# Hybrid decoder layer: norm weights of the mixers moved into the merge's split of y, D times x on ScalarE, the transposes of B in another PSUM bank, the SSM means one level later

## The chip, the cores and the metric

The kernel runs on one core of one Trainium2 chip: TensorE (PE), VectorE (DVE), ScalarE (ACT), GpSimd (POOL), and DMA queues issued by SP, ACT and POOL. The metric is the device time of one execution in microseconds. Lower is better.

## The reference

One layer over 1024 tokens of width 1024, float32. What matters here is the token mixer: three branches on the projection of the normed input, whose results are merged by gates and projected.

```python
o = chunked_gated_linear_attention(q, k, v, log_a, GLA_CHUNK)      # GLA; HGRN2 is the same form
o = rms_norm(o, gla_norm_w.reshape(GLA_HEADS, GLA_DV)).reshape(bsz, t_len, GLA_VW)
y_gla = (o * jax.nn.silu(gr.astype(f32))).astype(dtype)
...
y = ssd_chunked_scan(xs, dt, a_neg, bm, cm, SSM_CHUNK)
y = y + ssm_d.astype(f32)[:, None] * xs
y = y.reshape(bsz, t_len, SSM_D_INNER) * jax.nn.silu(sz.astype(f32))
y = rms_norm(y.reshape(..., SSM_GROUPS, SSM_D_INNER // SSM_GROUPS), ssm_norm_w.reshape(...))
...
merged = g0 * (y_gla @ w_br_gla) + g1 * (y_hgrn @ w_br_hgrn) + g2 * (y_ssm @ w_br_ssm)
return merged @ w_out
```

`rms_norm(x, w)` is x times the inverse root of its mean square, times w. In `ssd_chunked_scan` each chunk of 128 tokens uses `w = decay * (C B^T) * dt` within the chunk, and a state that is scaled and gets `x B^T` added. After the mixer come a second norm, the router, 32 experts (top 2 of a group) and a last norm.

## The kernel before, in words

The program is a row of blocks: the first norm and decays, `project` (the input projection), `mixers`, `merge_and_route`, the experts, `finish`. Each block has one hand-written list of instructions for each engine, and semaphores between them; each engine works through its own list in order, so a wait holds up all that stands behind it.

**`mixers` (578 to 1086 us)** goes over 8 chunks of 128 tokens (`body(c)`). Channels lie on partitions. GLA and HGRN2 are computed by levels: for level 0 to 6 VectorE makes two factor tiles (`factors`, L1468 to L1470), TensorE multiplies them (`level`, L1627), VectorE copies the wanted part into `score` (`scores_in`, L1486). The SSM branch has B and C in `bc_in`, x in `x_in` (named `gate_raw_a` in the trace, as z is), the decay matrix `wmat` (named `dn_raw_a`). `wmat` is loaded by SP as a broadcast of the 16 heads' b to all partitions (`load_bb`, L1128, 1 MB), as soon as TensorE has used the old one; VectorE's L1517 is the first to read it.

Between these, TensorE's list has gate matmuls: `fill(8)` puts eight of the 128x512 matmuls (L1602) that project the merge's gates. Each 24 of them make a result of 512 columns ("head") in PSUM bank 7, which ScalarE evicts (`late`, L1258) and stores; ScalarE also rounds the next gate weights (`late_hi`, L1251) or issues their load (L1246), and VectorE makes their remainder (`late_lo`, L1375).

Work of chunk c that is finished during chunk c+1, in VectorE's order: the norm of o with the gate (L1439, L1443), the sum of the parts of y (L1400), D times x (L1405), the gate z (L1411); then ScalarE squares it (`ssm_squares`, L1283), TensorE averages the squares over the channels by a matmul with a constant matrix (`ssm_means`, L1657, in two parts), ScalarE turns the mean into the inverse root (`ssm_scale`, L1287 and L1289), and VectorE forms the result (`ssm_out`, L1454). The weights of both norms and D are columns, one number for each partition and each 128 channels, so L1443, L1405 and L1454 are eight instructions each.

TensorE's list around the place in question, in chunk c: level 3, `ssm_state(c-1)` (L1649, reads B transposed, `bT`), eight gate matmuls, `ssm_means(c-1)` (L1657, into bank 2), the four transposes of B (L1701, into bank 6), eight gate matmuls, level 4, eight gate matmuls, the eight transposes of x (L1710, into banks 2 and 3), level 5. Bank 6 holds C B^T before, which VectorE reads by L1523 (`cbm`), so L1701 waits for `cbm_ready`. ScalarE copies B transposed to SBUF by L1330, late in the chunk. L1710 waits for `ms2_read`: ScalarE must have read the means from bank 2.

**`merge_and_route`** starts behind a barrier. It loads y for half of the tokens in eight pieces of two 512-column groups. ScalarE rounds a piece to the upper part (`upper_y`, L2118), VectorE makes the remainder (`rest_y`, L2217), and TensorE multiplies both parts with the branches' weights (L2457), starting with piece 0. The second half's pieces are split during the output projection (L2478).

Of the kernel before, what the change touches and what calls it, by code (L numbers as in the profile page):

```python
# [17 lines left out]
P = 128  # L18
T = 1024
D = 1024  # L20
CH = 128
# [936 lines left out]
def mixers(nc, io, dr, h_hi, h_lo, l_raw, l_hi, l_lo, w_place, xz_place, stored, early):  # L958
# [10 lines left out]
    N_PAR = 5  # L969
# [4 lines left out]
    with ExitStack() as ctx:  # L974
# [35 lines left out]
        nw, nw_s, d_col = sb("nw", [P, NH]), sb("nw_s", [P, 8]), sb("d_col", [P, 8])  # L1010
# [69 lines left out]
        intra_used = sem("intra_used")  # L1080
        xd_ready = sem("xd_ready")
# [21 lines left out]
        def _(sp):  # L1103
# [61 lines left out]
            sp.dma_start(nw[:, 0:4], io["gla_norm_w"].rearrange("(k p) -> p k", p=P)).then_inc(par_in, 16)  # L1165
            sp.dma_start(nw[:, 4:8], io["hgrn_norm_w"].rearrange("(k p) -> p k", p=P)).then_inc(par_in, 16)
            sp.dma_start(nw_s[:], io["ssm_norm_w"].rearrange("(k p) -> p k", p=P)).then_inc(par_in, 16)
# [72 lines left out]
        def _(act):  # L1240
# [37 lines left out]

            def ssm_squares(c):
# [11 lines left out]
            def body(c):  # L1291
# [23 lines left out]
                late(h0 + 1)  # L1315
                if c:
                    ssm_scale(c - 1)
# [9 lines left out]
                act.wait_ge(bT_ps_ready, c + 1)  # L1327
                if c:
                    act.wait_ge(hupd_ready, c)
# [38 lines left out]
        def _(dve):  # L1368
# [68 lines left out]
            def gla_hgrn_out(c):  # L1437
# [132 lines left out]
            for c in range(NCH):  # L1570
                if c == 1:
# [1597 lines left out]
```

## Time and profile before

| | before |
|---|---|
| median of 3 runs | 2035.61 us |
| range of the runs | 2033.6 to 2041.8 us |
| span of the profiled execution | 2040.4 us |
| TensorE busy in the span | 1925.7 us, 94% |
| VectorE busy | 1472.5 us, 72% |
| ScalarE busy | 1048.0 us, 51% |
| mean granted TensorE clock | 0.975 |

The profiled execution is one of the kernel's; its span runs from its first to its last instruction, and the page gives no other time for it. Busy time of TensorE is modelled (matmuls overlap), so that 94% is not 94% of its peak. The granted clock is a share of 2.4 GHz; 0.5 is 1.2 GHz. From 1300 us on the DMA engines are nearly always busy (the experts' weights), before that TensorE is. A wait is put down to the event that came last. In rows of the order of time the first number is the start and the second the time until the last end; a name like `gate_raw_a` is that of the buffer, which x, z and y share.

### The profile page before, as it was taken

How to read it: one execution, taken by the hardware profiler on the slowest of the kernel's cores; microseconds unless marked ns; L12 is line 12 of the kernel's file. 1: busy time of each engine (PE TensorE's matmuls, PEld its weight loads, DVE VectorE, ACT ScalarE, POOL GpSimd, SP SyncE). 2: the span in 40 equal slices, each digit the busy share in tenths (PEclk: the TensorE clock that was granted, in tenths of full speed). 3: DMA queues.
4: the chain of work that ended last, by engine and by line, in shares of the span. 5: the costliest groups of instructions: out<-in, count | busy, mean ns of one | idle time of the engine just before them, and what ended most of it. 6: DMA issues, size and time to landing. Idle time of an engine off the chain costs nothing. (4 is left out here: it accounts for less than half of the span.)

```text
span 2040.4 us, 26797 instructions
## 1 busy us (share of the span) xinstructions
PE 1925.7 (94%) x10602; PEld 1576.7 (77%) x10603; DVE 1472.5 (72%) x1687; ACT 1048.0 (51%) x1234; POOL 218.3 (11%) x173
## 2 busy tenths in 40 slices
PE   6999999999999999999998999995999999999993
PEld 5789888888977777777776888874788888888881
DVE  5876467667227888788775656556889988999875
ACT  5234344444224545444444334223777887888763
POOL 3310000000030000000001000012122222222210
PEclk9999999999999999999998999997999999999996
DMA  5242332432355557656537654543999999999986
GB/s 168 86 145 73 114 104 97 131 104 93 107 145 158 151 160 168 167 127 152 160 115 282 206 204 182 229 178 138 349 376 384 389 386 385 389 386 387 387 331 259
DMA packets 212415, 436.11 MB, mean 214 GB/s; under 512 B 28018, under 2 KB 151042, under 8 KB 184770
## 3 DMA queue, kind: packets, MB, share of 16 engines
q1 hardware_dynamic: 179394, 355.68, 50.3%
q10 hardware_dynamic: 20864, 53.49, 7.5%
q0 software_dynamic: 12032, 25.22, 3.2%
q8 instruction: 85, 1.39, 0.3%
q14 instruction: 40, 0.33, 0.0%
HBM read 369.67 MB, written 81.43 MB: 221 GB/s over the span
## 5 line engine op out<-in xcount | busy, mean ns | idle before, releaser
L1602 PE MATMUL psum<-h_hi,l_hi 128*128 128x512 f32 x384 | 158.5, 413 | 4.9 <-PEq L58 3.3
L1602 PE MATMUL psum<-h_lo,l_hi 128*128 128x512 f32 x384 | 159.8, 416 | 0.0
L1602 PE MATMUL psum<-h_hi,l_lo 128*128 128x512 f32 x384 | 157.9, 411 | 0.0
L2741 DVE TENSOR_TENSOR gu_lo<-up_raw,gu_hi 128x2048 fp32r<-128x2048 f32 x64 | 146.3, 2288 | 13.2 <-ACT gu_hi L2684 13.2
L2684 ACT CAST gu_hi<-up_raw 128x2048 fp32r<-128x2048 f32 x64 | 122.1, 1909 | 35.0 <-PE u_ps L2813 35.0
L1258 ACT COPY l_out<-psum 128x512 f32<-128x512 f32 x48 | 28.1, 585 | 170.3 <-PE psum L1602 162.3
L2457 PE MATMUL mpsum<-y_hi,wb_hi 128*128 128x512 f32 x256 | 103.3, 403 | 10.1 <-DVE y_lo L2217 9.1
L2813 PE MATMUL g_ps<-gu_hi,xeT_hi 128*128 128x512 f32 x256 | 105.0, 410 | 5.8 <-DVE xeT_lo L2750 5.8
L806 DVE TENSOR_TENSOR w_lo<-w_raw,w_hi 128x512 fp32r<-128x512 f32 x90 | 61.9, 689 | 65.5 <-ACT w_hi L662 65.5
L662 ACT CAST w_hi<-w_raw 128x512 fp32r<-128x512 f32 x90 | 55.7, 622 | 91.9 <-PE ps L931 91.4
L2457 PE MATMUL mpsum<-y_lo,wb_hi 128*128 128x512 f32 x256 | 101.7, 397 | 0.0
L2457 PE MATMUL mpsum<-y_hi,wb_lo 128*128 128x512 f32 x256 | 101.6, 397 | 0.0
L2813 PE MATMUL g_ps<-gu_hi,xeT_lo 128*128 128x512 f32 x256 | 101.6, 397 | 0.0
L2813 PE MATMUL g_ps<-gu_lo,xeT_hi 128*128 128x512 f32 x256 | 101.4, 396 | 0.0
L2813 PE MATMUL u_ps<-gu_hi,xeT_lo 128*128 128x512 f32 x256 | 99.7, 389 | 0.0
L2813 PE MATMUL u_ps<-gu_hi,xeT_hi 128*128 128x512 f32 x256 | 99.6, 389 | 0.0
L2813 PE MATMUL u_ps<-gu_lo,xeT_hi 128*128 128x512 f32 x256 | 99.6, 389 | 0.0
L3123 POOL DMA_INDIRECT xe<-s_h,recs x32 | 88.6, 2770 | 32.4 <-PE xT_ps L2784 14.9
L1602 PEld LDWEIGHTS psum<-h_hi,l_hi 128*128 128x128 f32 x384 | 73.2, 191 | 21.9 <-issue 7.0
L2741 DVE TENSOR_TENSOR gu_lo<-gate_raw_a,gu_hi 128x2048 fp32r<-128x2048 f32 x32 | 73.4, 2293 | 22.2 <-ACT gu_hi L2684 22.2
L1602 PEld LDWEIGHTS psum<-h_hi,l_lo 128*128 128x128 f32 x384 | 73.5, 191 | 18.8 <-issue 3.3
L2662 POOL DMA_INDIRECT s_pairs<-ye,recs x32 | 41.4, 1293 | 431.3 <-ACT ye L2701 417.9
(465 smaller groups left out, 5419.0 us busy)
## 6 DMA issues: line engine op xcount, KB each, us to landing
up_raw<-moe SPq DMA_DIRECT2D x62, 1024.0 KB, 8.1
gate_raw_a<-moe SPq DMA_DIRECT2D x33, 1024.0 KB, 8.4
gate_raw<-moe SPq DMA_DIRECT2D x33, 1024.0 KB, 8.4
dn_raw_a<-moe SPq DMA_DIRECT2D x31, 1024.0 KB, 7.2
dn_raw<-moe SPq DMA_DIRECT2D x31, 1024.0 KB, 8.0
w_raw<-w_in SPq DMA_DIRECT2D x26, 1024.0 KB, 6.1
l_raw<-w_gates ACTq DMA_DIRECT2D x24, 512.0 KB, 5.4
s_gates<-l_out ACTq DMA_DIRECT2D x48, 256.0 KB, 4.0
```

The source lines that it names most:

```text
L662: nc.scalar.copy(slot_hi[g], source(n, g)).then_inc(hi_ready, 1)
L806: ins = tt(slot_lo[g], source(n, g), slot_hi[g].bitcast(F32), ALU.subtract).then_inc(split_ready, 1)
L1258: nc.scalar.copy(l_out[h % 2][:], psum[:, late_bank(h), :]).then_inc(l_evicted, 1)
L1602: ins = nc.tensor.matmul(psum[:, bank, :], w[t % 2][:, k, :], x[:, k, half * 512:half * 512 + 512], start=i == 0, stop=i == LATE_MM - 1, s ...
L2457: ins = nc.tensor.matmul(ps[:, br, :], w[:, k * P:(k + 1) * P], y[:, k, :], start=k == k0 and q == 0, stop=k == k1 - 1 and q == 2)
L2662: pool.indirect_dma_start(out=dr["pairs"], out_offset=bass.IndirectOffsetOnAxis(ap=recs[:, e, 1:2], axis=0), in_=ye[b][:], in_offset=None, ...
L2684: nc.scalar.copy(gu_hi[p][:], gu_raw[p][:]).then_inc(gu_hi_ready, 1)
L2741: nc.vector.tensor_tensor(gu_lo[p][:], gu_raw[p][:], gu_hi[p][:].bitcast(F32), ALU.subtract).then_inc(gu_ready, 1)
L2813: ins = nc.tensor.matmul(ps[:], x[:, (p - at) * GK + k, :], w[:, k, :], start=p == at and k == 0 and q == 0, stop=p == at + GU // 2 - 1 an ...
L3123: nc.gpsimd.indirect_dma_start(out=xe[e % 2][:], out_offset=None, in_=dr["h2"], in_offset=bass.IndirectOffsetOnAxis(ap=recs[:, e, 0:1], ax ...
```

## The change

- The weights of the GLA, HGRN2 and SSM norms leave the mixers. L1443 and L1454 become one multiplication of 1024 columns each. The weights are loaded into `y_weight`, a tile that lives on, and are applied where the merge splits y: the rounding on ScalarE takes them as its scale, the remainder on VectorE as its scalar. A piece is now two instructions of 512 columns on each of the two engines.
- D times x moves from VectorE (L1405) to ScalarE (`x_scaled`): eight activations in place in `x_in`, once x has been transposed. VectorE adds the product by one instruction.
- B is transposed into the second half of `mid_ps` (bank 3), not bank 6. L1701's wait for `cbm_ready` goes; a wait for `ms_read` comes. The copy of `bT` on ScalarE moves ahead of `ssm_scale`, and the wait for `bT_ready` on TensorE moves from `intra` to the transposes of x.
- `ssm_means` moves on TensorE from ahead of the transposes of B to behind level 4.

```diff
+            for (k0, k1), name in (((0, 4), "gla_norm_w"), ((4, 8), "hgrn_norm_w"), ((8, 16), "ssm_norm_w")):
+                sp.dma_start(y_weight[:, k0:k1], io[name].rearrange("(k p) -> p k", p=P)).then_inc(early["yw"], 16)
...
+            def x_scaled(c):
+                if c == 0:
+                    act.wait_ge(par_in, 16 * N_PAR)
+                act.wait_ge(xT_ready, c + 1)
+                for k in range(8):
+                    ins = nc.scalar.activation(x_in[:, k, :], x_in[:, k, :], ACT.Copy, scale=d_col[:, k:k + 1])
+                ins.then_inc(xs_ready, 1)
...
                 late(h0 + 1)
+                act.wait_ge(bT_ps_ready, c + 1)
+                if c:
+                    act.wait_ge(hupd_ready, c)
+                nc.scalar.copy(flat(bT[:]), mid_ps[:, 512:1024]).then_inc(bT_ready, 1)
                 if c:
                     ssm_scale(c - 1)
...
-                nc.scalar.copy(flat(bT[:]), ssm_ps).then_inc(bT_ready, 1)
...
                 late(h0 + 3)
+                x_scaled(c)
...
             def x_in_sum(c):
                 dve.wait_ge(intra_used, 2 * c + 2)
-                for k in range(8):
-                    ins = stt(yt[:, k, :], x_in[:, k, :], d_col[:, k:k + 1], yt[:, k, :], ALU.mult, ALU.add)
-                ins.then_inc(xd_ready, 1)
+                dve.wait_ge(xs_ready, c + 1)
+                tt(yt[:], x_in, yt[:], ALU.add).then_inc(xd_ready, 1)
...
-                for h in range(NH):
-                    ins = stt(ya[:, h, :], g_in[:, h, :], nw[:, h:h + 1], ya[:, h, :], ALU.mult, ALU.mult)
-                ins.then_inc(ya_ready, 1)
+                tt(ya, g_in[:], ya, ALU.mult).then_inc(ya_ready, 1)
...
-                for k in range(8):
-                    ins = stt(yb[:, k, :], yt[:, k, :], nw_s[:, k:k + 1], rs2[:, k // 2, :], ALU.mult, ALU.mult)
-                ins.then_inc(yb_ready, 1)
+                grouped = lambda x: x.rearrange("p (g a) t -> p g a t", a=2)
+                tt(grouped(yb), grouped(yt[:]), rs2[:].unsqueeze(2).to_broadcast([P, SSM_GROUPS, 2, CH]), ALU.mult).then_inc(yb_ready, 1)
...
                 fill(SLOT)
                 if c:
-                    ssm_means(c - 1)
-                pe.wait_ge(cbm_ready, c + 1)
+                    pe.wait_ge(ms_read, c)
                 for g in range(SSM_GROUPS):
-                    ins = nc.tensor.transpose(ssm_ps[:, g * P:(g + 1) * P], bc_in[:, g, :], ident[:])
+                    ins = nc.tensor.transpose(mid_ps[:, 512 + g * P:512 + (g + 1) * P], bc_in[:, g, :], ident[:])
                 ins.then_inc(bT_ps_ready, 1)
                 fill(SLOT)
                 level(c, 4)
+                if c:
+                    ssm_means(c - 1)
                 fill(SLOT)
                 pe.wait_ge(x_loaded, 16 * (c + 1))
+                pe.wait_ge(bT_ready, c + 1)
...
-                nc.scalar.copy(y_hi[:, q * PK:(q + 1) * PK, :], y_part(p)).then_inc(y_hi_ready, 1)
+                for a in range(PK):
+                    k = q * PK + a
+                    ins = nc.scalar.activation(y_hi[:, k, :], y_part(p)[:, a, :], ACT.Copy, scale=y_weight[:, k:k + 1])
+                ins.then_inc(y_hi_ready, 1)
...
-                tt(y_lo[:, ks, :], y_part(p), y_hi[:, ks, :].bitcast(F32), ALU.subtract).then_inc(y_ready, 1)
+                for a in range(PK):
+                    k = q * PK + a
+                    ins = stt(y_lo[:, k, :], y_part(p)[:, a, :], y_weight[:, k:k + 1], y_hi[:, k, :].bitcast(F32), ALU.mult, ALU.subtract)
+                ins.then_inc(y_ready, 1)
```

TensorE in the middle of a chunk, from level 3's last part to the transposes of x; the gate matmuls between are left out. Before:

```order
L1649 MATMUL psum<-xdt,bT 128x256 x3
...
L1657 MATMUL psum<-y_out,mean_b 128x512 [waits ms_read,sq2_ready]
L1657 MATMUL psum<-y_out,mean_b 128x512
L1701 MATMUL psum<-ident_m,bc_in 128x128 [waits cbm_ready]
L1701 MATMUL psum<-ident_m,bc_in 128x128 x3
...
L1627 MATMUL psum<-q_lv,k_lv 64x2x32 [waits score_ready,qk_ready]
...
L1710 MATMUL psum<-ident_m,gate_raw_a 128x128 [waits ms2_read,x_loaded]
```

And now:

```order
L1702 MATMUL psum<-ident_m,bc_in 128x128 [waits ms_read]
L1702 MATMUL psum<-ident_m,bc_in 128x128 x3
...
L1630 MATMUL psum<-q_lv,k_lv 64x2x32 [waits score_ready,qk_ready]
...
L1660 MATMUL psum<-y_out,mean_b 128x512 [waits ms_read,sq2_ready]
L1660 MATMUL psum<-y_out,mean_b 128x512
L1605 MATMUL psum<-h_hi,l_hi 128x512 [waits l_evicted,l_split]
...
L1714 MATMUL psum<-ident_m,gate_raw_a 128x128 [waits ms2_read,bT_ready,x_loaded]
```

The means stand behind level 4, right ahead of the gate matmuls that begin a new head, and L1714 has one wait more.

ScalarE in the same part of a chunk with an even number, from the differences (L1310) on. Before:

```order
L1258 COPY l_out<-psum 128x512 [waits l_stored0,l_done]
L1260 DMA s_gates<-l_out 128x512 [waits l_evicted]
L1246 DMA l_raw<-w_gates 128x1024 [waits l_split]
L1287 ACTIVATE rs<-psum,eps 128x512 [waits ms2_ready]
L1289 ACTIVATE rs<-rs 128x512 [waits ms2_read]
...
L1330 COPY bT<-psum 128x512 [waits hupd_ready,bT_ps_ready]
...
L1246 DMA l_raw<-w_gates 128x1024 [waits l_split]
L1337 ACTIVATE y_out<-psum 128x1024 [waits ya_stored,o_ready]
```

And now:

```order
L1258 COPY l_out<-psum 128x512 [waits l_stored0,l_done]
L1260 DMA s_gates<-l_out 128x512 [waits l_evicted]
L1246 DMA l_raw<-w_gates 128x1024 [waits l_split]
L1327 COPY bT<-psum 128x512 [waits hupd_ready,bT_ps_ready]
L1295 ACTIVATE rs<-psum,eps 128x512 [waits ms2_ready]
L1297 ACTIVATE rs<-rs 128x512 [waits ms2_read]
...
L1284 ACTIVATE gate_raw_a<-gate_raw_a,d_col 128x128 [waits xT_ready]
L1284 ACTIVATE gate_raw_a<-gate_raw_a,d_col 128x128 x7
L1346 ACTIVATE y_out<-psum 128x1024 [waits ya_stored,o_ready]
```

The copy of B stands ahead of the two instructions of `ssm_scale`, and D's eight stand ahead of the squares of o. `yt` and `y_out` are y before and after its norm, `rs` the inverse roots.

## Rows read from the trace of the kernel before

**Rows 1.** Waits of TensorE, 577 to 1100 us: total us, times, longest.

```profile
PE psum L1657 <- ACT y_out L1283: 9.6, 4, 2.4
PE psum L1701 <- DVE cbm L1523: 9.1, 4, 2.8
PE mpsum L2457 <- DVE y_lo L2217: 9.1, 1, 9.1
```

**Rows 2.** TensorE in order of time, chunk 4: start, us, line, operands, idle before.

```profile
853.05 0.39 PE L1602 MATMUL psum<-h_hi,l_hi 128*128 128x512 f32 x1
853.28 1.88 PE L1657 MATMUL psum<-y_out,mean_b 128*128 128x512 f32 x4
857.96 0.66 PE L1701 MATMUL psum<-ident_m,bc_in 128*128 128x128 f32 x4 [2.80 <-DVE cbm L1523]
...
864.72 1.04 PE L1710 MATMUL psum<-ident_m,gate_raw_a 128*128 128x128 f32 x8
```

**Rows 3.** Windows of chunks 1 to 7: length, PE busy (instructions), granted clock, DMA.

```profile
853.28:864.72 11.44, 8.64 (x49) 0.85 1.00 289
...
1027.80:1037.52 9.72, 7.31 (x49) 1.00 0.98 297
sum 77.35, PE 58.66; mean PE 8.38
```

**Rows 4.** The same columns: windows of chunk 0 and of the last means.

```profile
626.57:628.97 2.40, 2.40 (x14) 1.00 0.87 200
628.97:631.76 2.79, 2.79 (x34) 1.00 0.58 102
1072.90:1074.21 1.31, 1.31 (x5) 1.00 0.83 300
```

**Rows 5.** b: issue in order of time, landings by line, VectorE's wait (us, times, longest).

```profile
837.05 0.36 SPq L1128 DMA_DIRECT2D dn_raw_a<-s_b_ssm  x1
...
DMA to landing us min/median/max: 14.8/16.0/18.4
...
DVE wd L1517 <- DMA dn_raw_a<-s_b_ssm: 5.8, 4, 2.0
```

**Rows 6.** VectorE in order of time, chunk 4.

```profile
850.69 1.22 DVE L1411 TENSOR_TENSOR yt<-yt,gate_raw_a 128x1024 f32<-128x1024 f32 x1
853.33 0.18 DVE L1517 TENSOR_TENSOR wd<-dn_raw_a,b_dt 128x16 f32<-128x16 f32 x1 [1.41 <-DMA dn_raw_a<-s_b_ssm]
...
855.62 0.55 DVE L1470 TENSOR_TENSOR q_lv<-q_in,ex 128x384 f32<-128x384 f32 x1
...
857.23 0.68 DVE L1523 TENSOR_TENSOR cbm<-psum,tri 128x512 f32<-128x512 f32 x1
```

**Rows 7.** Groups by line and form, 577 to 1110 us: busy us, mean ns, idle.

```profile
L1310 ACT ACTIVATE dn_raw_a<-dn_raw_a,b_dt 128x128 f32<-128x128 f32 x128 | 39.1, 387 | 0.3
...
L1443 DVE SCALAR_TENSOR_TENSOR y_out<-g_in,nw,y_out 128x128 f32<-128x128 f32 x64 | 17.5, 349 | 0.9
...
L1330 ACT COPY bT<-psum 128x512 f32<-128x512 f32 x8 | 4.5, 565 | 0.0
```

**Rows 8.** ScalarE in order of time, chunk 4.

```profile
854.86 2.45 ACT L1310 ACTIVATE dn_raw_a<-dn_raw_a,b_dt 128x128 f32<-128x128 f32 x8
861.75 0.59 ACT L1258 COPY l_out<-psum 128x512 f32<-128x512 f32 x1 [4.45 <-PE psum L1602]
...
863.37 0.69 ACT L1287 ACTIVATE rs<-psum,eps 128x512 f32<-128x512 f32 x1 [1.03 <-issue]
```

**Rows 9.** ScalarE and VectorE at the end of chunk 4.

```profile
884.40 0.51 ACT L1271 ACTIVATE ex<-ex 128x384 f32<-128x384 f32 x1
...
890.36 0.56 DVE L1468 TENSOR_TENSOR k_lv<-k_in,ex 128x384 f32<-128x384 f32 x1
```

**Rows 10.** ScalarE and VectorE in order of time, start of the merge.

```profile
1092.23 1.99 ACT L2118 CAST y_hi<-gate_raw_a 128x1024 fp32r<-128x1024 f32 x2
...
1093.63 2.44 DVE L2217 TENSOR_TENSOR y_lo<-gate_raw_a,y_hi 128x1024 fp32r<-128x1024 f32 x2
```

More of the change, by code:

```diff
@@ L955, in late_bank, with mixers @@
     return 7
-def mixers(nc, io, dr, h_hi, h_lo, l_raw, l_hi, l_lo, w_place, xz_place, stored, early):
+def mixers(nc, io, dr, h_hi, h_lo, l_raw, l_hi, l_lo, w_place, xz_place, y_weight, stored, early):
     LEVELS = [64 >> n for n in range(7)]
@@ L968, in mixers @@
     NH = GLA_HEADS + HG_HEADS
-    N_PAR = 5
+    N_PAR = 2
     HALF = P // 2
@@ L1009, in mixers @@
         eps = sb("eps", [P, 1])
-        nw, nw_s, d_col = sb("nw", [P, NH]), sb("nw_s", [P, 8]), sb("d_col", [P, 8])
+        d_col = sb("d_col", [P, 8])
         psum = ctx.enter_context(nc.psum_tensor("psum", [P, 8, 512], F32))
@@ L1080, in mixers @@
         intra_used = sem("intra_used")
+        xs_ready = sem("xs_ready")
         xd_ready = sem("xd_ready")
@@ L1164, in _ @@
             load_g(0)
-            sp.dma_start(nw[:, 0:4], io["gla_norm_w"].rearrange("(k p) -> p k", p=P)).then_inc(par_in, 16)
-            sp.dma_start(nw[:, 4:8], io["hgrn_norm_w"].rearrange("(k p) -> p k", p=P)).then_inc(par_in, 16)
-            sp.dma_start(nw_s[:], io["ssm_norm_w"].rearrange("(k p) -> p k", p=P)).then_inc(par_in, 16)
             for a in range(2):
@@ L1326, in body @@
                 nc.scalar.activation(wmat, wmat, ACT.Exp, scale=-1.0).then_inc(wexp_ready, 1)
-                act.wait_ge(bT_ps_ready, c + 1)
-                if c:
-                    act.wait_ge(hupd_ready, c)
-                nc.scalar.copy(flat(bT[:]), ssm_ps).then_inc(bT_ready, 1)
                 act.wait_ge(kT_ps_ready, c + 1)
@@ L1570, in _ @@
             for c in range(NCH):
-                if c == 1:
-                    dve.wait_ge(par_in, 16 * N_PAR)
                 body(c)
@@ L1662, in intra @@
                     pe.wait_ge(w_ready, c + 1)
-                    pe.wait_ge(bT_ready, c + 1)
                 else:
@@ L1783, in piece, with merge_and_route @@
     return io["moe"][e, p].rearrange("p (k f) -> p k f", k=GK if p < GU else DK)
-def merge_and_route(nc, io, dr, ident, w_raw, y_raw, up_raw, up_at, xe, recs, recs_in, gather, early, kept_sem):
+def merge_and_route(nc, io, dr, ident, w_raw, y_raw, y_weight, up_raw, up_at, xe, recs, recs_in, gather, early, kept_sem):
     HT = T // 2
@@ L2155, in _ @@
             upper_w0(first, w0_loaded, w0_hi_ready)
+            act.wait_ge(early["yw"], 48)
             for p in range(4):
@@ L2215, in rest_y @@
                 q = p % PIECES
-                ks = slice(q * PK, (q + 1) * PK)
-                tt(y_lo[:, ks, :], y_part(p), y_hi[:, ks, :].bitcast(F32), ALU.subtract).then_inc(y_ready, 1)
+                for a in range(PK):
+                    k = q * PK + a
+                    ins = stt(y_lo[:, k, :], y_part(p)[:, a, :], y_weight[:, k:k + 1], y_hi[:, k, :].bitcast(F32), ALU.mult, ALU.subtract)
+                ins.then_inc(y_ready, 1)
             def gated(n):
@@ L2319, in _ @@
             rest_w0(first, w0_hi_ready, w0_ready)
+            dve.wait_ge(early["yw"], 48)
             for p in range(4):
@@ L3092, in build @@
         dn_first, gate_first = many(1, "dn_raw_a", [P, DK, D]), many(1, "gate_raw_a", [P, GK, FF])
-        early = {name: kept_sem(f"early_{name}") for name in ("w0", "w0_rest", "y0", "y1")}
+        early = {name: kept_sem(f"early_{name}") for name in ("w0", "w0_rest", "y0", "y1", "yw")}
+        y_weight = ctx.enter_context(nc.sbuf_tensor("y_weight", [P, 2 * KT], F32, side="right"))
         with ExitStack() as front:
@@ L3107, in build @@
             l_raw, l_hi, l_lo = ([l[:, b] for b in range(2)] for l in late_parts)
-            mixers(nc, io, dr, h_hi, h_lo, l_raw, l_hi, l_lo, flat(dn_first[0]), flat(gate_first[0]), stored, early)
+            mixers(nc, io, dr, h_hi, h_lo, l_raw, l_hi, l_lo, flat(dn_first[0]), flat(gate_first[0]), y_weight, stored, early)
         ident = ctx.enter_context(nc.sbuf_tensor("ident", [P, P], F32))
@@ L3125, in gather @@
                                          bounds_check=T - 1, oob_is_err=False).then_inc(gathered[e % 2], 16)
-        merge_and_route(nc, io, dr, ident, dn_raw, gate_raw, up_raw, up_at, xe, recs, recs_in, gather, early, kept_sem)
+        merge_and_route(nc, io, dr, ident, dn_raw, gate_raw, y_weight, up_raw, up_at, xe, recs, recs_in, gather, early, kept_sem)
         x2_kept = many(KEPT, "x2_kept", [P, D])
```

## The prediction, made before the changed kernel was timed

> **What bounds the kernel now.** I read first the sum of waits on TensorE over the mixer stage, then TensorE in order of time around the longest wait, then the windows that hold each such place, then VectorE, ScalarE and the DMA issues at one of them. From 578 to 1086 us TensorE is the engine that always has work, and it has two kinds of wait left, 9.6 us before the SSM means (L1657) and 9.1 us before the transposes of B (L1701) [rows 1]. Both stand at one place of each chunk: between the end of the eight gate matmuls behind the state update and the transposes of x (L1710).
>
> Chunk 4 shows it [rows 2]. The last gate matmul starts at 853.05; these start 0.23 apart, so TensorE could go on at 853.28, and the means do. The transposes of B come only at 857.96, after 2.80 us of idle time, and the x transposes only at 864.72. I measure the stretch from the end of those gate matmuls to L1710. In the seven chunks that have it, it is 9.72 to 11.44 us, together 77.35 [rows 3]. Five of the seven windows have a mean granted clock of 0.85 (full for most of it, at 1.2 GHz for part), the other two 1.00. Chunk 7 is one of the two: it waited 2.4 us, kept 2.4 GHz and took 9.72; chunk 4 waited 0.4 longer, dipped and took 11.44, so one dip costs some 1.3 to 1.7 us on top of its wait; I take 1.5.
>
> What the same instructions take with nothing in their way: in chunk 0 the transposes and gate matmuls 2.40 us, level 4 and gate matmuls 2.79, and at the end of the stage the means 1.31, all at a clock of 1.00 [rows 4]. That is 6.50 a chunk, 45.5 for seven. The waits and dips together cost 77.35 - 45.5 = 31.85 us, and that is all that the change can win here. Outside of this place it touches the seam to the merge, where TensorE waits 9.1 us once [rows 1].
>
> **Part 1: VectorE gets shorter.** Three sets of eight scalar_tensor_tensor of 128 columns become one tensor_tensor of 1024 each. A set takes 17.5/8 = 2.19 us [rows 7], the single one 1.22 (L1411 has that form, [rows 6]): 0.97 less each. Two sets (norm weights of GLA/HGRN, and D) stand ahead of the stall, so the gated yt is ready 1.9 us sooner; the third is behind it. None of this reaches TensorE in full: right behind them VectorE has to have b, the 1 MB broadcast into wmat, for L1517. In chunk 4 it is issued at 837.05 and L1517 starts at 853.33, when it landed; VectorE waited for it in four chunks, 5.8 us together, and it lands 14.8 to 18.4 us after its issue (in chunks 1 to 7 15.8, 16.0, 14.9, 16.3, 18.4, 16.1, 14.8) [rows 5]. **This load, not VectorE, is what is late next.**
>
> **Part 2: the new order on TensorE.** The transposes of B go to a bank of their own and no longer wait for cbm. TensorE ends the gate matmuls 853.28 - 837.05 = 16.23 us after the issue of b [rows 2, 5], and about the same in all seven. It then does the transposes and eight gate matmuls without asking VectorE for anything new, 2.40 us [rows 4]. It stands at level 4 at 18.63 after the issue. Level 4 needs the factors that end with the L1470 at 855.62 + 0.55, that is 2.84 us after L1517 began [rows 6]; with the semaphore I take 2.9. So the new stall is landing + 2.9 - 18.63: 0.1, 0.3, 0, 0.6, 2.7, 0.4 and 0, together 4.1 us. The largest one is chunk 5 with its 18.4. Stalls under 1 us should leave the clock alone (a 2.4 us one did in chunk 7).
>
> The means come after level 4. What they read, the squares, was ready at 853 in chunk 4 and would be earlier; level 4 ends near 857. No wait is left there.
>
> The chain behind the means is new: the x transposes must wait for both the copy of B and the logarithm that reads the means. ScalarE gets through the differences at 854.86 + 2.45, that is 3.98 after L1517; then it evicts a gate bank and has its queue (1.62 us from L1258 to L1287 in even chunks, [rows 8]), copies B in 0.565 (hidden before, L1330 in [rows 7]), and takes 0.69 for the logarithm: landing + 6.9. TensorE, if it had to wait at level 4, arrives at landing + 2.9 + 2.79 + 1.31 = landing + 7.0. So it fits, by 0.1. In odd chunks the gate's rounding stands there (1.05 us in place of the load's issue) and the chain is 7.35; TensorE waits 0.3 where b was late. I charge 0.6 for the stage. The next gate head needs the evicted bank two matmul groups earlier, near landing + 5.0 (7.0 less some 2.0 for its own eight), and has it at landing + 3.98 + 0.59 = 4.6.
>
> Later in the chunk everything moves up with it: level 5 needs the factors 9.5 us after L1517 at the latest (two levels' scores, the state's two steps and a gate remainder stand between, all of sizes that it does today), and TensorE asks near 9.9.
>
> **Part 3: D on ScalarE.** Eight activations of 128 columns with a column as scale. The nearest row is L1310, same shape, with a column as bias: eight in 2.45 us [rows 8], 0.387 each and overlapping [rows 7]. They stand where ScalarE is about to square o. In chunk 4 the last activation there ends at 884.40 + 0.51 = 884.91, and VectorE takes its result at 890.36 [rows 9]; 2.45 us go into a slack of 5.4. Cost zero; without that cover it would be 8 x 2.45 = 19.6 us. On the queues: the norm weights and D still are five small loads on SP ahead of chunk 0's first wait, only in another order, and no later load moves past another.
>
> **Part 4: the split of y at the seam.** A piece is one copy of 1024 columns on ScalarE (two in 1.99) and one subtraction on VectorE (two in 2.44) [rows 10]. Now each is two instructions of 512. Bounds: no more than today, and twice the fixed part. An eight-piece row costs 2.19 where one costs 1.22 [rows 7, 6], so a further instruction costs 0.14 us on VectorE. On ScalarE eight of 128 take 2.45 where 1024 columns take 1.0 [rows 8, 10], so 0.2 each. Only the first piece stands before TensorE's start: 0 to 0.4 us, I take 0.3. The others run ahead of TensorE, which needs 1.4 us or more for a piece. The second half's pieces lie under the output projection.
>
> The Trainium skill, "ScalarE: Activation LUTs" (the section on ACTIVATE's rate), has a column operand cost about 93 ns more than an immediate; its estimate for 128 columns is also the 387 ns of the row, and for a piece it would make 1.23 us of 0.95. By that the first piece costs 0.3 too.
>
> **The sum.** 31.85 - 4.1 - 0.6 - 0.3 = 26.9 us. On the profiled execution: 2040.4 - 26.9 = 2013.5. That execution is 4.8 above the median of the runs shown and inside their range (2033.6 to 2041.8); nothing in the trace says where the 4.8 lie. On the median: 2035.6 - 26.9 = **2008.7**.
>
> **Rivals.**
> - *b lands later.* The gated yt comes 1.9 us sooner, and it releases the loads of x and z on SP's queue and, in odd chunks, through the gate remainder, a 512 KB load on ScalarE's queue. Today these start just as b lands; then they would run beside its last 2 us. Chunk 5 speaks for it (b at 18.4), chunks 1 to 4, 6 and 7 had no such case. If odd chunks land at 18.4, they stall 2.7 + 0.3 each, 12.0 in all, the even ones 1.3: gain 31.85 - 13.3 - 0.3 = 18.3, or 2017; with dips in them 1.5 x 4 more, 2023. The Trainium skill, "DMA: Bandwidth & Descriptors" (arbitration), says that an engine takes turns between the queues that have work for it, which speaks for this rival; of the traces here only chunk 5's landing bears on it.
> - *All of it goes.* b lands at 14.8 to 16.0 each time: the stalls are gone, gain 31.5, 2004.
> - *Little comes.* The stall only moves, to level 4 and to the x transposes, with the dips: five stalls of 2.5 and five dips of 1.5 leave 31.85 - 20 = 12, and anything worse is within 0.5%: 2024 to 2036.
> - *Slower.* D's eight activations on ScalarE hold up its squares and the next chunk's exponentials, for which VectorE waits at L1468. It decides from the point where the eight take the whole slack of 5.4 us; it is a loss against the 26.9 won from 5.4 + 26.9/8 = 8.8 us, 1.1 us for each. At 1.3 each it is 8 x (10.4 - 5.4) - 26.9 = 13.1 lost: 2049. The row of 0.387 speaks against.
>
> **How the numbers follow.** Forecast 0.60 (2004 to 2014), b later 0.20, all of it 0.10, little 0.07, slower 0.03. The range takes in the forecast, the gain in full (down to the fastest run, 2002), and most of the later b: 2002 to 2021. A measurement of this kernel can tell about 0.5%, 10 us. Faster by more than that: 0.60 + 0.20 + 0.10 + 0.01 = 0.91; within it 0.06; slower 0.03.
>
> **What would show it.** In the changed kernel: the same stretch near 6.5 to 7.2 us in six chunks with a granted clock of 1.00; no wait of TensorE on cbm or on the squares, and in their place short ones of level 4 on q_lv; L1517's counterpart waiting for b in every chunk; the eight activations in about 2.45 us with no new wait of VectorE at the start of a chunk; the merge's first wait 9.1 to 9.5. It would be wrong if b landed at over 17 in most chunks, if the x transposes waited for ScalarE's logarithm by over 1 us, or if the clock dipped elsewhere.

## The result, and the profile after

| | before | changed |
|---|---|---|
| median | 2036.06 us | 2025.7 us |
| range | 2033.6 to 2041.8 | 2024.6 to 2026.2 |
| ratio, 95% interval | | 0.9943 [0.9929, 0.9956] |
| span of the profiled execution | 2040.4 us | 2024.5 us |
| VectorE busy | 1472.5 us | 1449.7 us |
| ScalarE busy | 1048.0 us | 1071.0 us |
| first x transposes to the merge's first matmul | 463.3 us | 445.0 us |
| stretch, seven chunks | 77.35 us | 59.65 us |

The run of before has one time more than the table ahead of the prediction. The forecast was 2008.7, with a range of 2002 to 2021. The kernel became faster by 10.4 us where 26.9 were expected, and its time is outside the range. The two profiled executions differ by more, 2040.4 - 2024.5 = 15.9 us: the one of before took 2041.8 us, the longest of its four and 5.7 above their median, the changed one 2026.2, 0.5 above its own. So of the 16.5 us that are missing the profiles can explain 11.0; the other 5.5 are, but for some tenths, the place of the two executions among their runs. The prediction read its 31.85 us from a long execution and took the gain off the median; what made that execution long is open. "Stretch" is the prediction's: from the end of the eight gate matmuls behind the state update to the transposes of x.

The waits of TensorE over the mixers, by line, as us in total, times and longest (the counterpart of [rows 1]):

```profile
PE mpsum L2468 <- DVE y_lo L2226: 9.3, 1, 9.3
PE psum L1630 <- DVE q_lv L1475: 8.2, 5, 2.1
...
PE psum L1714 <- ACT rs L1295: 0.8, 2, 0.4
PE psum L1714 <- ACT bT L1327: 0.6, 1, 0.6
```

The two waits of before, 9.6 on the squares and 9.1 on cbm, are gone, as forecast. In their place TensorE waits 8.2 us at level 4 for its factor `q_lv`, twice the 4.1 that the prediction had. The merge's first wait went from 9.1 to 9.3; the price of the split at the seam was 0.2.

The same windows as in [rows 3], of which chunks 1, 2, 4 and 6 are shown (length, PE busy, granted clock, DMA share and GB/s):

```profile
682.86:691.74 8.88, 6.96 (x49) 1.00 1.07 329
738.55:747.65 9.10, 6.97 (x50) 1.00 1.00 291
...
848.77:859.48 10.71, 8.66 (x49) 0.84 1.08 323
...
960.61:969.13 8.52, 6.95 (x49) 1.00 0.98 284
...
sum 59.65, PE 50.65; mean PE 7.24
```

None of the seven is within the 6.5 to 7.2 us that the prediction gave as a sign. Chunk 4 is again the longest, and the only one with a lower clock. TensorE in it, in order of time, without the gate matmuls that are alike (the counterpart of [rows 2]):

```profile
848.77 0.60 PE L1702 MATMUL psum<-ident_m,bc_in 128*128 128x128 f32 x4
...
853.29 0.89 PE L1630 MATMUL psum<-q_lv,k_lv 128*64 128x64 f32 x24 [2.05 <-DVE q_lv L1475]
854.11 3.64 PE L1660 MATMUL psum<-y_out,mean_b 128*128 128x512 f32 x4
856.76 1.26 PE L1605 MATMUL psum<-h_hi,l_hi 128*128 128x512 f32 x1
...
859.48 1.03 PE L1714 MATMUL psum<-ident_m,gate_raw_a 128*128 128x128 f32 x8
```

VectorE and SP at the same place, in order of time, b's landings by its line, and VectorE's wait for it (the counterparts of [rows 5, 6]):

```profile
844.18 1.22 DVE L1419 TENSOR_TENSOR yt<-yt,gate_raw_a 128x1024 f32<-128x1024 f32 x1
850.38 0.18 DVE L1522 TENSOR_TENSOR wd<-dn_raw_a,b_dt 128x16 f32<-128x16 f32 x1 [4.97 <-DMA dn_raw_a<-s_b_ssm]
```

```profile
832.58 0.37 SPq L1129 DMA_DIRECT2D dn_raw_a<-s_b_ssm  x1
845.43 0.36 SPq L1133 DMA_DIRECT2D gate_raw_a<-s_xbc  x1
...
846.48 4.59 SPq L1195 DMA_DIRECT2D s_y<-y_out  x1
```

```profile
DMA to landing us min/median/max: 14.7/17.5/18.3
```

```profile
DVE wd L1522 <- DMA dn_raw_a<-s_b_ssm: 20.4, 7, 5.0
```

VectorE has the gated yt at 845.40, and SP issues x at once. b, issued at 832.58, lands 17.8 us later, at 850.38; VectorE sat idle for it for 4.97 us, 20.4 in all against 5.8 before. Level 4 starts 2.91 us after that landing. The median landing went from 16.0 to 17.5. And the loads of x and z follow b by 12.9 us, where it was 14.9 before (851.94 against the issue at 837.05 of [rows 5]): they now start while b is still under way. Four of the seven landings are over 17 us, which is one of the signs that the prediction gave for being wrong.

Behind the wait of 2.05 us the clock falls: the window's mean is 0.84, and the means take 856.76 - 854.11 = 2.65 us to the next matmul, where they took 1.42 in another run at full clock (e9, below).

Where the 17.7 us of the stretch went short of the forecast: it was to be 77.35 - 31.85 + 4.7 = 50.2 and is 59.65. Of the 9.5 between, 4.1 are the longer wait for b, 0.8 the two small waits before L1714 (1.4 in place of 0.6), 1.7 the dip of chunk 4 (59.65 less all else), and 2.9 a unit that was too small, 6.50 where it is 6.91 (shown below). Outside of the stretch the stage is the same to 0.6 us (463.3 - 77.35 = 385.95, now 385.35), while the rest of the program takes 2.4 more (1577.1 and 1579.5).

### The profile page after: what moved, and what is told of

It reads as the page before. It is cut to its first block and busy times, and to the rows that moved or that the text cites. A ratio compares the mean times of both kernels' runs of the same rounds, so it can differ in the third digit from the quotient of the medians.

```text
span 2024.5 us, 26730 instructions
## 1 busy us (share of the span) xinstructions
PE 1920.6 (95%) x10602; PEld 1576.5 (78%) x10603; DVE 1449.7 (72%) x1535; ACT 1071.0 (53%) x1314; POOL 216.1 (11%) x173
## 5 line engine op out<-in xcount | busy, mean ns | idle before, releaser
L1258 ACT COPY l_out<-psum 128x512 f32<-128x512 f32 x48 | 28.0, 583 | 139.9 <-PE psum L1605 133.7
L1605 PEld LDWEIGHTS psum<-h_lo,l_hi 128*128 128x128 f32 x384 | 73.1, 190 | 18.1 <-issue 3.6
```

The lines of the kernel that those rows point to most:

```text
L1258: nc.scalar.copy(l_out[h % 2][:], psum[:, late_bank(h), :]).then_inc(l_evicted, 1)
L1605: ins = nc.tensor.matmul(psum[:, bank, :], w[t % 2][:, k, :], x[:, k, half * 512:half * 512 + 512], start=i == 0, stop=i == LATE_MM - 1, s ...
```

## The experiments

The theory after the result: **b's load is the bound behind VectorE, and a sooner VectorE makes b itself land later**, because SP issues x, z and the store of y while b is on its way. The rivals: the lower clock is the whole of it; VectorE's own work ahead of level 4 is; ScalarE's new work is. All ratios are to before on the same chip.

The profiles of all runs side by side (stage: first x transposes to the merge's first matmul; landing: b's mean over chunks 1 to 7, from its issue; x: its issue behind that of b; us):

| run | ratio | stage | stretch | landing | x |
|---|---|---|---|---|---|
| before | | 463.3 | 77.35 | 16.0 | 14.8 to 15.3 |
| e1_before_again | 0.9996 | 462.7 | 76.71 | 16.1 | 14.8 to 15.3 |
| changed | 0.9943 | 445.0 | 59.65 | 16.7 | 12.8 to 13.6 |
| e2_after_again | 0.9920 | 452.3 | 66.91 | 17.0 | 12.8 to 13.6 |
| e10_after_third | 0.9931 | 448.3 | 62.99 | 17.0 | 12.8 to 13.6 |
| e3_hold_xz | 0.9889 | 443.4 | 58.00 | 16.0 | 14.7 to 18.6 |
| e4_order_only | 0.9923 | 446.2 | 60.25 | 15.8 | 14.8 to 15.3 |
| e5_vector_only | 1.0020 | 467.3 | 81.97 | 17.3 | 12.9 to 13.6 |
| e6_wd_later | 0.9914 | 450.6 | 62.16 | 17.3 | 12.8 to 13.6 |
| e7_b_off_path | 0.9975 | 458.3 | 48.37 | 17.3 | 12.9 to 13.6 |
| e8_b_off_old_vector | 0.9997 | 460.1 | 50.18 | 16.8 | 14.8 to 15.3 |
| e9_b_off_evict | 0.9872 | 438.7 | 51.80 | 18.4 | 12.8 to 13.6 |
| e11_b_off_evict_hold | 0.9960 | 452.3 | 63.56 | 17.2 | 19.9 to 20.5 |
| e12_evict_old_vector | 0.9917 | 443.8 | 50.10 | 18.2 | 15.3 to 18.4 |

### The two kernels again: e1, e2, e10

> The kernel before, unchanged, for a second profile. The first profiled execution was 4.8 us above the median of its runs. Theory A (the mixers' stalls are the same in every execution and the 4.8 us lie elsewhere): the stretch from the end of the gate matmuls to the transposes of x sums to 77 +-1 us over chunks 1 to 7 again, and the span is near 2035. Theory B (the 4.8 us were clock dips in the mixers): the stretch sums to about 73.

> The changed kernel, unchanged, for a second profile. Theory A: b lands later because x, z and y's store are issued sooner; then the seven landings are again 14.7 to 17.9 us with four of them over 17, and the waits of TensorE at level 4 sum to 8 us. Theory B (those landings were chance, as the 18.4 us of chunk 5 in the kernel before): they change places and sum, to 4 us or less. In the first 140 us: the dip of the clock between 80 and 100 us is there again if it belongs to the kernel, and gone if it is chance.

> The changed kernel itself, on the same chip as the two others of this call. Every theory: within 3 us of 2025.7, ratio to before 0.992 to 0.995; stretch 58 to 68 us, according to how many of its waits at level 4 (8 to 10 us together) are followed by half-clock matmuls.

Before once more: 0.9996 [0.9978, 1.0014], stretch 76.71, as theory A said; but its profiled execution was a long one again (2043.1, 5.0 above its median), so whether the stretch is shorter in an execution near the median stays open. The dip of the clock between 80 and 100 us belongs to no kernel: the mean clock there was 1.00 and 0.83 in the two profiles of before, and 0.83, 0.91 and 0.91 in those of the changed kernel. The changed kernel: 0.9920 [0.9891, 0.9949] and 0.9931 [0.9911, 0.9952], that is 13.5 and 11.5 us less, with stretches of 66.91 and 62.99. In e2 again four landings are over 17 (up to 18.5), and the waits at level 4 are 10.0 where 8 was expected. What differs between its three profiles is above all the clock. Sum and mean of the seven windows of e2, and its longest chunk:

```profile
903.08:914.50 11.42, 8.63 (x49) 0.85 1.06 318
...
sum 66.91, PE 55.75; mean PE 7.96
```

Four chunks had a clock of 0.84 to 0.85 in e2, two in e10, one in the profile shown above. Of the waits at level 4 and what followed: 1.95 (e2), 2.05, 2.09, 2.19, 2.26, 2.69 and 2.79 us dipped; 1.92, 2.12 and 2.57 did not. A wait of about 2 us is a toss.

Over the three profiles the stretch is 63.2 on average. Against the forecast's 50.2 that is 13.0 too much: 5.3 of waits at level 4 (8.2, 10.0 and 10.1, where 4.1 were forecast), 2.9 of the unit, 0.6 before the x transposes, and what is left, 4.2, are dips (seven, so 1.8 each).

### Holding x and z back: e3

```diff
                     sp.wait_ge(yt_ready, c + 1)
+                    sp.wait_ge(wdarg_ready, n + 1)
                     load_x(n)
```

> The changed kernel, but SP issues the loads of x and z, and all behind them, only once VectorE has read b (one more wait on SP, on wdarg_ready). If x, z and y's store delay b: b lands 14.8 to 16.3 us after its issue in the even chunks too (17.3 to 17.9 before this edit), TensorE's waits at level 4 fall from 8.2 to under 3 us, and the time falls by about 5 us, unless x then comes late for its transposes (its load takes 4 to 5 us, its transposes come 7 us after b's landing). If the landings are chance or due to ScalarE's queue: still over 17 in some chunks, same time.

SP issues x, z and the store of y only when VectorE has read b. Result 0.9889 [0.9849, 0.9930], 2019.67 against 2025.35 of e2 on the same chip. b's landings and the waits of TensorE:

```profile
DMA to landing us min/median/max: 14.4/16.1/18.3
```

```profile
PE psum L1631 <- DVE q_lv L1476: 4.1, 3, 2.6
```

```profile
900.17:912.82 12.65, 10.07 (x49) 0.73 0.92 282
```

The landings of chunks 1 to 7 are 14.9, 16.7, 15.3, 15.9, 18.3, 16.3 and 14.4, on average 16.0, as before (16.0 there, and 16.1 in e1); in the three profiles of the changed kernel they were 16.7, 17.0 and 17.0. The wait at level 4 is 4.1, the size that the prediction had given it. It is not under the 3 us of the expectation, and one landing is over 17; the time is 5.7 us less, as expected, but the two intervals overlap. e3 is one profile, so I set all of them beside each other. In chunks 2, 4 and 6 of the five profiles with x at 12.8 to 13.6 and ScalarE's order unchanged up to the differences (changed, e2, e10, e5, e6) b lands at 17.1 to 19.0; in the four with x later (before, e1, e3, e4) at 15.6 to 17.6. In chunks 3 and 7 it lands at 14.4 to 15.9 in all nine, so x's place moves it in some chunks and not in others; why is open. Since e3 differs from the changed kernel only in SP's wait, what SP issues behind b is the cause of the later landing there. Which of the three transfers it is was not taken apart. One of the stalls was left, chunk 5 with its landing at 18.3: a wait of 2.58 and a stretch of 12.65 at a clock of 0.73, so this one cost 3.2 on top of its wait.

What that does to b shows in the DMA views. The columns are packets, MB and the time of the packets as a share of 16 engines. From just behind b's issue to its landing in chunk 4, the queue q1 of before, the same of the changed kernel, and then the changed kernel from 842 to 845, when b is alone:

```profile
q1 hardware_dynamic: 2137, 1.13, 51.7%
```

```profile
q1 hardware_dynamic: 2906, 1.49, 28.7%
```

```profile
DMA packets 366, 0.19 MB, mean 62 GB/s; under 512 B 0, under 2 KB 366, under 8 KB 366
...
q1 hardware_dynamic: 366, 0.19, 19.8%
```

b has 2048 packets of 512 bytes. Before, q1 moved 2137 until b had landed, so nearly nothing but b. In the changed kernel it moved 2906, that is 0.36 MB more. SP had issued nothing else on that queue than x, z and, from 846.48 on, y's store, so these 0.36 MB are theirs, and they moved before b had landed. The other queue, q10, moved the same (0.82 MB and 0.79). And b alone crawls, at 62 GB/s, with a fifth of the engines' time. In before, from 841 to 849, b alone moved 77 GB/s and its packets took 68% of that time, so the busy share says little about its rate. What makes it so slow, or lets later packets move before it is in, no run shows. Nor is x the only thing that moves b: in the first nine rows of the table x's place separates the means, 15.8 to 16.1 against 16.7 to 17.3, but e8 and e12 land at 16.8 and 18.2 with x at 15 and more, and e11 at 17.2 on average although x is issued only once b has landed. ScalarE's transfers stand elsewhere in those; that was not taken apart.

### The parts alone: e4 and e5

> The kernel before with the second half of the change alone: transposes of B in the other bank and without the wait for cbm, copy of B ahead of ssm_scale, means behind level 4. VectorE's work, the norm weights, D and the merge are as before. x and z are then issued when they were before, so b should land at 14.8 to 16.3 (one outlier). Theory A (the order brings the gain, b's load takes part of it back in the full change): time about 1 to 4 us below the full change or equal to it, stretch sum 52 to 58 us. Theory B (VectorE's shorter work is needed): stretch sum over 65.

e4 is before with the new order on TensorE, the new bank and the earlier copy of B; norm weights, D and the split of y are as before. 0.9923 [0.9898, 0.9947], 2021.63. Its waits and the sum of its windows:

```profile
PE psum L1602 <- ACT l_out L1258: 4.8, 5, 1.1
PE psum L1627 <- DVE q_lv L1470: 3.5, 6, 1.1
...
PE psum L1711 <- ACT rs L1287: 1.9, 4, 0.5
```

```profile
sum 60.25, PE 50.48; mean PE 7.21
```

All seven chunks kept a clock of 1.00. **The order part gives the whole gain.** VectorE is ready later by its 1.9 us, and b lands sooner by about 1 (15.8 on average), so level 4 waits no longer than in the changed kernel, 3.5 us; 4.8 and 1.9 go to small waits on the eviction and on the logarithm. So theory A holds in its time, but the stretch of 60.25 is over the 52 to 58 that it gave.

> The changed kernel with the old order: B transposed into bank 6 behind the wait for cbm, means ahead of it, copy of B late. What is left of the change is the shorter work on VectorE, D on ScalarE and the weights in the merge. Theory A (this part alone wins nothing, since b's load is right behind it and lands later): TensorE does the means at once, then waits for cbm, which comes 3.9 us after b's landing (5.1 in even chunks); the stretch sums to 72 to 80 us and the time is within 5 us of the kernel before. Theory B (VectorE was the bound): the stretch falls to under 65 and the time by over 10 us.

e5 is the other half: the changed kernel with the order, bank and copy of before. 1.0020 [1.0005, 1.0036].

```profile
PE psum L1704 <- DVE cbm L1528: 19.7, 7, 4.8
...
PE psum L1660 <- ACT y_out L1291: 2.4, 4, 0.8
```

VectorE is 3 us shorter in each chunk, and the kernel is not faster: cbm stands behind the read of b, b lands at 17.3 on average, and the wait on cbm goes from 9.1 to 19.7 us; the wait on the squares, which VectorE does set, goes from 9.6 to 2.4. The stretch of 81.97 is above even theory A's 72 to 80. The prediction's words "none of this reaches TensorE in full" were too mild: alone, this part costs 4 us of the stage.

### Level 4's factors ahead of the read of b: e6

```diff
-                dve.wait_ge(bb_loaded, 16 * (c + 1))
-                dve.wait_ge(tok_ready, 1)
-                tt(wd[b][:, 0, :], wmat[:, :, CH - 1], tok[:, c, 0, :], ALU.subtract).then_inc(wdarg_ready, 1)
                 scores_in(2)
                 dec(i0 + 6)
                 factors(4)
+                dve.wait_ge(bb_loaded, 16 * (c + 1))
+                dve.wait_ge(tok_ready, 1)
+                tt(wd[b][:, 0, :], wmat[:, :, CH - 1], tok[:, c, 0, :], ALU.subtract).then_inc(wdarg_ready, 1)
```

> The changed kernel; VectorE's read of b (the argument of wd) moves behind the factors of level 4. Theory A (b's landing holds level 4 only because VectorE reads it first): TensorE's waits at level 4 go from 8 to 10 us to under 1. The same landing still holds ScalarE's chain (differences, evicting the gate bank, copy of B, logarithm), so waits of 1 to 2 us appear behind level 4, at the gate matmuls (L1605) or the x transposes; the stretch sums to 54 to 60 us and the time is 0 to 6 us below the changed kernel. Theory B (VectorE itself is late there): the waits at level 4 stay over 5 us.

0.9914 [0.9884, 0.9944]. The wait at level 4 is gone, and 9.5 us on the eviction of a gate bank have come:

```profile
PE psum L1605 <- ACT l_out L1258: 9.5, 8, 2.8
```

ScalarE's list has eight differences ahead of that eviction (`late(h0 + 1)`), and they need b. VectorE does the same work ahead of level 4 as in the changed kernel but for the read of b, so it was that read and not its own work that held level 4. The new waits are longer than expected (up to 2.8 us for 1 to 2) and the stretch is 62.16 for 54 to 60; three of its windows have a lower clock.

### b behind everything in the stretch: e7 and e8

In e7 the read of b stands behind the factors of levels 4 and 5 on VectorE, and on ScalarE all 16 differences behind the copy of B and `ssm_scale`, ahead of the eviction of the third head. e8 is the same on e4's base, that is with the norm weights and D on VectorE.

> The changed kernel with b off both paths: VectorE reads it behind the state update, and ScalarE evicts the gate bank, copies B, takes the logarithm and makes level 6's exponentials before it touches b (then wd, the exponentials of eb and all sixteen differences). Theory A (b's landing is all that holds the stretch): no wait over 0.5 us is left in it, it takes 6.9 us in every chunk and 48 to 50 us in sum, clock 1.00 in the seven windows, time 10 to 14 us below the changed kernel. Theory B (other work is as late as b): the sum stays over 55.

> The kernel with the new order alone (VectorE, D, weights and merge as before), with b off both paths in the same way. It tells what the shorter work on VectorE is worth once b does not hide it. Theory A (little: VectorE ends level 4's factors 18.9 us after b's issue in odd chunks, TensorE asks at 18.6): stretch 49 to 52 us in sum, time within 4 us of the run with both. Theory B (VectorE's 1.9 us a chunk count in full): stretch over 58 us, time over 8 us above it.

e7 gave 0.9975 [0.9959, 0.9991], e8 0.9997 [0.9983, 1.0012]. In e7 the stretch is what was wanted, 6.91 in every chunk; this is also the unit that the prediction had at 6.50. And then TensorE waits at the next bank. The waits, the windows' sum, and TensorE in order of time behind level 6 of chunk 4:

```profile
PE psum L1604 <- ACT l_out L1258: 18.4, 10, 2.2
```

```profile
sum 48.37, PE 48.37; mean PE 6.91
```

```profile
867.57 0.48 PE L1604 MATMUL psum<-h_hi,l_hi 128*128 128x512 f32 x1 [2.06 <-ACT l_out L1258]
...
869.21 0.63 PE L1604 MATMUL psum<-h_hi,l_hi 128*128 128x512 f32 x1
869.64 0.63 PE L1604 MATMUL psum<-h_lo,l_hi 128*128 128x512 f32 x1
```

So 77.35 - 48.37 = 29.0 us are won in the stretch, and 24.0 lost elsewhere in the stage (458.3 - 48.37 = 409.9, before 385.95): 18.4 of them waits for L1258, ten times up to 2.2 us, and the rest goes with matmuls at 1.2 GHz, such as those from 869.21 on, which start 0.43 apart and not 0.23. The stretch was forecast and the time was not: e7 was to be 10 to 14 us below the changed kernel, and by the ratio it is above it (0.9975 against 0.992 to 0.994).

e8's stretch is 50.18, with 1.4 us of waits for `q_lv`, as theory A had it. Its time is neither theory's: the medians, from ten runs each on one chip, are 2035.66 in e7 and 2041.88 in e8, 6.2 us apart (4 and 8 were the bounds). Their stages are only 1.8 apart in the profiles. So the shorter VectorE is worth something once b is out of the way; where, these two profiles don't show.

### The eviction ahead of the differences as well: e9, e11, e12

ScalarE in e9, a chunk's middle:

```diff
                 relative(c, 6)
+                i = NE * c + NL
+                act.wait_ge(d_ready, i + 1)
+                nc.scalar.activation(ex[i % 3][:], ex[i % 3][:], ACT.Exp).then_inc(e_ready, 1)
+                nc.scalar.activation(b_in[b][:], b_in[b][:], ACT.Exp).then_inc(eb6_ready, 1)
                 act.wait_ge(wdarg_ready, c + 1)
...
                 nc.scalar.activation(eb_in[:], eb_in[:], ACT.Exp).then_inc(small_ready, 1)
+                late(h0 + 2)
                 act.wait_ge(small_ready, c + 1)
                 differences(range(SSM_HEADS))
```

> The changed kernel with b's first readers moved behind level 4's and 5's factors, and on ScalarE the eviction of the third gate head ahead of the sixteen differences instead of behind them. In e7_b_off_path the stretch was 6.91 us in every chunk, but TensorE then waited 18.4 us in ten places for that eviction. Theory (b's landing sets the stall, and in e7 only ScalarE's order gave the gain back): stretch 48 to 49 us in seven chunks, the wait on l_out from 18.4 to under 2 us, first x transposes to merge 434 to 437 us, time 10 to 14 us below the changed kernel, near 2012. Rival (VectorE and ScalarE are so full that the wait only moves again): a new wait of 8 us or more in the second half of a chunk, before the weights by C (w), before intra or before the transposes of k, and a time within 4 us of the changed kernel's.

**0.9872 [0.9845, 0.9899], 2017.77 us, 9.8 below e10 on the same chip**: the fastest version here.

```profile
PE psum L1713 <- DMA gate_raw_a<-s_xbc: 3.3, 1, 3.3
...
PE psum L1604 <- ACT l_out L1258: 0.3, 1, 0.3
```

```profile
894.52:904.86 10.34, 7.08 (x49) 1.00 0.80 255
...
sum 51.80, PE 48.54; mean PE 6.93
```

```profile
896.92 0.89 PE L1629 MATMUL psum<-q_lv,k_lv 128*64 128x64 f32 x24
897.74 1.99 PE L1659 MATMUL psum<-y_out,mean_b 128*128 128x512 f32 x4
899.16 0.80 PE L1604 MATMUL psum<-h_hi,l_hi 128*128 128x512 f32 x1
899.79 0.40 PE L1604 MATMUL psum<-h_lo,l_hi 128*128 128x512 f32 x1
...
904.86 1.29 PE L1713 MATMUL psum<-ident_m,gate_raw_a 128*128 128x128 f32 x8 [3.27 <-DMA gate_raw_a<-s_xbc]
```

```profile
891.68 0.36 SPq L1133 DMA_DIRECT2D gate_raw_a<-s_xbc  x1
```

The wait on `l_out` is 0.3. Six chunks are at 6.91, 51.80 in all with the seventh; chunk 5 waits 3.3 us for x. b landed 20.7 us after its issue there, and x, issued at 891.68 behind it on the same queue, 13 us after its own, where it took 7 to 9 in the other six. That looks like the old cause at a new place; it is not shown. The stage takes 438.7 us, where 434 to 437 were expected, and the time is 9.8 us less for 10 to 14, so the theory is right and its figures are missed by little.

> As e9, and in addition SP issues the loads of x and z only once VectorE has read b. If b's landing no longer stands before anything of TensorE, the hold has nothing left to give: within 3 us of e9, stretch again 48 to 49 us. If b's landing still decides something (the differences, and through them the weights by C), it is 3 to 6 us faster than e9. Too late a load of x would show as a wait of TensorE before the x transposes.

0.9960 [0.9943, 0.9977]. The hold of e3, now tied to a read of b that comes much later, sends x 20 us after b (e3: 15 to 19, e9: 13), and TensorE waits for it in every chunk, 13.1 us:

```profile
PE psum L1714 <- DMA gate_raw_a<-s_xbc: 13.1, 7, 3.1
```

b lands at 17.2 on average against 18.4 in e9, which hardly anything waits for in either. This is the miss that the expectation's last sentence names. Loads issued when b is nearly in, and not when it has been read, should avoid both; no run tried it.

> As e9_b_off_evict, but from the kernel with only the new order and bank: norm weights and D on VectorE as before, old split of y. What VectorE's 3 us less a chunk are worth once neither b nor the eviction stands in TensorE's way. If nothing (they were hidden behind b in the changed kernel and are hidden behind gate matmuls here): within 5 us of e9's ratio 0.987, stretch 48 to 51, no wait over 1 us on cbm, q_lv or the squares. If VectorE becomes the bound without them: new waits of 1 us or more a chunk on cbm or on a level's factors, 8 us or more slower than e9, ratio 0.991 or above.

0.9917 [0.9893, 0.9941]. The stretch is 50.1 with no dip in it, yet the stage is 443.8 us against 438.7 in e9.

```profile
PE psum L1626 <- DVE q_lv L1469: 5.9, 7, 2.7
```

```profile
838.66 1.31 PE L1626 MATMUL psum<-q_lv,k_lv 128*64 128x64 f32 x24 [2.72 <-DVE q_lv L1469]
```

The 5.9 us of waits for `q_lv` are mostly at an earlier level, in even chunks (2.72 at 838.66). By the ratio it is the second case, by the waits a smaller one. With b away VectorE is the bound that its shortening was meant for, and the shortening, with what comes with it (D on ScalarE, the new split), is worth 5.1 us by the profiles. The medians were taken on two chips and their intervals meet, so they add little to that; e7 and e8, on one chip, are 6.2 us apart the same way.

## Why the prediction was wrong, point by point

- **What bounds the kernel, and the place: right.** Both waits went; all but 0.6 us of the stage's gain is in the stretch.
- **"This load, not VectorE, is what is late next": right**, and the formula too. Landing + 2.9 - 18.63 with the landings measured (17.6, 17.8, 15.4, 17.8, 16.3, 17.3, 14.7) gives 1.9, 2.1, 0, 2.1, 0.6, 1.6 and 0, together 8.3; measured 8.2.
- **The landings put into it: wrong, and this is the step that failed.** The sum kept 15.8 to 18.4 as they were, though the same paragraph had VectorE ready 1.9 us sooner and the next loads of SP wait for just that. The case was seen, as the rival "b lands later", and held at 0.20. Its places were wrong as well: it put the late landings into the odd chunks, by ScalarE's load. They came in 1, 2, 4 and 6 here, in 2, 4, 5 and 6 in e2, and e3, which holds SP's transfers only, takes them away but for chunk 5's. In its place: landings of 16.7 to 17.0 on average, not 16.0, and 8.2 to 10.1 us of waits at level 4, not 4.1.
- **No dips: wrong.** The sum charges none, not even behind its largest stall of 2.7, and it leans on chunk 7, where a wait of 2.41 kept the clock. In the same trace chunks 1 and 3 waited 2.41 as well and had a clock of 0.85. Chunks 1 and 7, the waits and the windows:

```profile
681.22 3.65 PE L1657 MATMUL psum<-y_out,mean_b 128*128 128x512 f32 x4 [2.41 <-ACT y_out L1283]
...
1030.38 1.98 PE L1657 MATMUL psum<-y_out,mean_b 128*128 128x512 f32 x4 [2.41 <-ACT y_out L1283]
```

  The window of chunk 1 is 11.43 us, that of chunk 3 11.33 and that of chunk 7 9.72, so a dip costs 1.6 to 1.7 at the same wait, where 1.5 was taken. With 8 to 10 us of waits, most of about 2, one to four chunks dip, 4.2 us on average. The rival had 6 us for four dips, in odd chunks; they came in chunks 2, 4, 5 and 6.
- **The unit of 6.50: 0.41 too small, 2.9 in all.** It was put together from pieces of chunk 0 and of the stage's end; e7 and e9 show the whole. In the last rows of e9 level 4 takes 0.82 and the means 1.42 (forecast 1.31), and the eight gate matmuls behind the means take 6.91 - 2.40 - 0.82 - 1.42 = 2.27 (forecast 2.79 - 0.82 = 1.97): behind the means the first of them takes 0.63 to the next, not 0.23. A sum of pieces misses what an instruction costs behind another neighbour. [rows 3] could have warned of it: chunk 7's window, all at full clock, has 7.31 us of busy time in the old order, not 6.50.
- **The x transposes: 1.4 for 0.6.** Right mechanism, small.
- **D on ScalarE at no cost: right.** Eight activations at 387 ns, as forecast, and VectorE's wait for the exponentials at a chunk's start didn't grow (L1473: 14.6 us in 4, before L1468: 19.2 in 10).

```profile
L1284 ACT ACTIVATE gate_raw_a<-gate_raw_a,d_col x64: 384/387/402, 651.4 to 1040.5; 128x128 f32<-128x128 f32 x64
```

```profile
DVE k_lv L1473 <- ACT ex L1271: 14.6, 4, 5.7
```

```profile
DVE k_lv L1468 <- ACT ex L1271: 19.2, 10, 7.1
```

- **The seam: 0.2 for 0.3.** Right. On ScalarE the four instructions of two pieces take 2.55 us, where the two took 1.99, so 0.3 more a piece.
- **The range.** Its top of 2021 lies between the rival alone (2017) and the rival with its dips (2023), and the measured 2025.7 is above both. With the means of the three profiles the sum is 31.85 - 9.4 (level 4) - 1.2 (before the x transposes) - 4.2 (dips) - 2.9 (unit) - 0.2 (seam) = 13.9, which gives 2021.7. That is near the gains of 13.5 and 11.5 of e2 and e10; the 4.0 that it lacks here are of the part that the profiles don't explain. The errors were not independent: a later b brings both the longer wait and the dips.
- **The rule on turns.** The rival came true, but the rows don't bear out the reason that it was given: b, x and z are all on q1, and q10 carried as much as before. The Trainium skill, "DMA: Bandwidth & Descriptors" (arbitration), speaks of turns between queue rows, and so has no bearing on b and x, which share one.

## What to carry to other kernels

When a bound is a DMA landing, ask what the edit makes start sooner on the same queue, and charge the landing with it. Look for cases in your own trace that speak against a reading: two waits of 2.41 us with a dip stood beside the one without. Price the two halves of an edit apart: here the order gave all of the gain and the shorter VectorE gave none until b's readers had moved, after which it gave some 5 us. Take the gain off the time of the execution that it was read from, and say how far that one is from the median. A wait moved off one place shows up at the next one in the same engine's list (e6, e7), so a move wants its whole list read, up to the first instruction that needs nothing of it.

## What was not expected of the hardware

- A 1 MB broadcast load in 512-byte packets took 14.4 to 20.7 us. Alone it moved 62 to 77 GB/s, while its packets took 20 to 68% of the DMA engines' time. Transfers issued 2 us sooner behind it on the same queue moved its landing by about 1 us on average, and 0.36 MB of them moved before it had landed.
- TensorE waits of the same length differ in what follows: of three of 2.41 us in one trace two had matmuls at 1.2 GHz behind them and one had none; 2.12 and 2.57 us stayed at full clock, 1.95 and 2.05 did not. A dip cost 1.6 to 3.2 us beyond its wait.
